# A hybrid decoder block: the mixer's projections in three products of high and low halves, and the recurrence's gate products inside the second branch

## The reference, cut to what matters

```python
h = rmsnorm(x, norm_mix_g)
q, k, v, xr, yr, ga, gl = split_cols(h @ w_in)      # 512, 128, 128, 512, 512, 1024, 1024
y_attn = sliding_window_attention(rope(q), rope(k), v, sinks) @ w_attn_o
xr = causal_depthwise_conv(xr, conv_w, conv_b)
r, i = sigmoid(xr @ w_rg + b_rg), sigmoid(xr @ w_ig + b_ig)   # 64-wide diagonal blocks
log_a = -8 * r * softplus(-lam)
h_t = exp(log_a) * h_{t-1} + sqrt(1 - exp(2 * log_a)) * (i * xr)
y_lru = (h_t * gelu(yr)) @ w_lru_o
x = x + (sigmoid(ga) * y_attn + sigmoid(gl) * y_lru) @ w_out
x = x + moe(rmsnorm(x, norm_ffn_g), ...)             # top 4 of 32 experts
return rmsnorm(x, norm_final_g)
```

## Time and profile before

| | before |
|---|---|
| median of three runs | 2228.98 us (2228.72 to 2231.96) |
| the profiled execution, its own time | 2230.49 us |
| its span in the trace | 2228.9 us |
| busy: PE / PEld / DVE / ACT / POOL | 94% / 67% / 70% / 56% / 13% |
| mean granted clock of TensorE | 0.97 |

### The profile page before, as it was taken

The page is one execution under the profiler, slowest core; times in us unless marked ns, Lnnn a source line. Parts: engine busy times, 40 slices in busy tenths (PEclk is TensorE's granted clock), DMA queues, the critical chain, the costliest instruction groups (busy, mean ns, idle before and its releaser), DMA issues.

```text
span 2228.9 us, 36027 instructions
## 1 busy us (share of the span) xinstructions
PE 2088.0 (94%) x11352; PEld 1494.9 (67%) x11353; DVE 1550.9 (70%) x1964; ACT 1244.1 (56%) x1655; POOL 291.4 (13%) x334
## 2 busy tenths in 40 slices
PE   7989988999989749999999999999999999999993
PEld 4445555767668637777777777777777777777772
DVE  4326654555443448878877778987877998977894
ACT  3152434334333336766766657766766776765674
POOL 3010000000002420211212200111210110220000
PEclk9998999999999869999999999999999999999997
DMA  7110020110143476988988779978979979977994
GB/s 225 38 38 0 22 76 1 38 39 1 38 151 133 142 196 224 371 284 287 377 282 282 256 260 380 373 270 291 370 259 325 372 276 368 356 258 246 378 342 159
DMA packets 247678, 489.51 MB, mean 220 GB/s; under 512 B 19915, under 2 KB 29991, under 8 KB 247536
## 3 DMA queue, kind: packets, MB, share of 16 engines
q1 hardware_dynamic: 218768, 439.37, 54.7%
q0 software_dynamic: 21088, 49.35, 8.4%
q10 hardware_dynamic: 7776, 0.19, 0.2%
HBM read 461.01 MB, written 32.05 MB: 221 GB/s over the span
## 4 chain that ended last, share of the span: by engine, by line
PE 84%; DVE 5%; issue 4%; ACT 2%; DMA 2%; SPq 1%; POOL 0%; ACTq 0%; DVEq 0%; POOLq 0%
PE psum L650 14%; PE psum L651 14%; PE psum L654 14%; PE psum L667 8%; PE psum L423 5%; PE psum L548 5%; PE psum L536 3%; PE psum L538 3%; PE psum L531 3%; PE psum L638 2%; PE psum L447 2%; PE psum L491 2%; PE psum L593 1%; PE psum L617 1%; PE psum L594 1%
## 5 line engine op out<-in xcount | busy, mean ns | idle before, releaser
L1451 DVE TENSOR_TENSOR w_lo<-ring,w_hi 128x1024 fp32r<-128x1024 f32 x768 | 915.0, 1221 | 144.2 <-ACT w_hi L890 132.7
L890 ACT ACTIVATE w_hi<-ring 128x1024 fp32r<-128x1024 f32 x768 | 803.7, 1059 | 277.7 <-PE psum L654 269.0
L650 PE MATMUL psum<-w_hi,rows_hi 128*128 128x512 f32 x1024 | 422.6, 413 | 4.3 <-DVE rows_lo L1455 2.5
L651 PE MATMUL psum<-w_hi,rows_lo 128*128 128x512 f32 x1024 | 400.4, 391 | 0.0
L654 PE MATMUL psum<-w_lo,rows_hi 128*128 128x512 f32 x1024 | 316.6, 390 | 0.0
L650 PEld LDWEIGHTS psum<-w_hi,rows_hi 128*128 128x128 f32 x1024 | 194.1, 190 | 47.0 <-issue 10.5
L654 PEld LDWEIGHTS psum<-w_lo,rows_hi 128*128 128x128 f32 x1024 | 192.7, 188 | 41.3
L650 PE MATMUL psum<-w_hi,act_hi 128*128 128x512 f32 x512 | 219.9, 429 | 0.0
L651 PEld LDWEIGHTS psum<-w_hi,rows_lo 128*128 128x128 f32 x1024 | 193.5, 189 | 37.7
L651 PE MATMUL psum<-w_hi,act_lo 128*128 128x512 f32 x512 | 202.7, 396 | 0.0
L667 PE MATMUL psum<-ring,region_m 128*32 128x256 f32 x3072 | 174.2, 380 | 0.0
(11 more groups left out here) (286 smaller groups left out, 2596.0 us busy)
## 6 DMA issues: line engine op xcount, KB each, us to landing
ring<-in_w_gate_up_dram SPq DMA_DIRECT2D x128, 2048.0 KB, 15.9
ring<-in_w_down_dram SPq DMA_DIRECT2D x64, 2048.0 KB, 12.0
ring<-in_w_in_dram SPq DMA_DIRECT2D x9, 1024.0 KB, 8.2
ring<-in_w_in_dram SPq DMA_DIRECT2D x3, 2048.0 KB, 22.6
region_m<-in_x_dram SPq DMA_DIRECT2D x8, 512.0 KB, 9.7
ring<-in_w_out_dram SPq DMA_DIRECT2D x2, 2048.0 KB, 7.7
region_a<-in_x_dram POOLq DMA_DIRECT2D x8, 512.0 KB, 4.8
acc_rows<-region_a POOLq DMA_DIRECT2D x8, 512.0 KB, 2.9
```

The costliest lines, as they stand in the source:

```text
L650: mm(bank(i), hi[:, ks], wh, start=(k0 + q == 0), stop=False)
L651: mm(bank(i), lo[:, ks], wh, start=False, stop=False)
L890: act.activation(w_hi[:, n % NBUF, :], place[i][:, k0 * HALF:(k0 + 2) * HALF], ACT.Copy).then_inc(hi_done, 1)
L1451: v.tensor_tensor(out=w_lo[:, n % NBUF, :], in0=place[i][:, k0 * HALF:(k0 + 2) * HALF], in1=w_hi[:, n % NBUF, :].bitcast(f32), op=ALU.subt ...
```

## The change

The input, turned, is kept as two fp32r tiles hT_hi and hT_lo for the whole mixer, without the gain; the gain goes into the weights when these are split (`in_high`, `in_low`, for w_in's columns of xr, yr, k/v, q and the merge gates). So the merge gates no longer split the input again for each piece. Branches, q, k, v and the two output projections now go through `three`. The weights of xr are loaded between tiles 3 and 4, the first four xr groups (tokens 0 to 511) stand between the turns of tiles 4 to 7, and the weights of q are loaded only when all 32 groups are done. The 16 recurrence gate products are now n = 12 to 27, inside yr (8 to 11, 28 to 31). The decay stands inside step s = 1 of the attention's loop, the recurrence in s = 1 and 2. The output projections are split on the fly, in pieces p (16 for each j) through a ring of OBUF = 3 tiles. Staging the experts' biases (`bias_part`) moves from the merge gates' stage to w_out's.

```diff
+OBUF = 3
+RG_AT = 12
...
+            def three(dst, w_hi_, w_lo_, m_hi_, m_lo_, first, final):
+                mm(dst, w_hi_, m_hi_, start=first, stop=False)
+                mm(dst, w_hi_, m_lo_, start=False, stop=False)
+                return mm(dst, w_lo_, m_hi_, start=False, stop=final)
...
             sp.dma_start(wxr_sb, w_in_v[:, :, OFF_XR:OFF_XR + LW]).then_inc(wxr_in, 16)
+            tiles(NT // 2, NT)
             sp.dma_start(wyr_sb, w_in_v[:, :, OFF_YR:OFF_YR + LW]).then_inc(wyr_in, 16)
+            sp.wait_ge(branch_mm, 8)
+            sp.dma_start(wkv_sb, w_in_v[:, :, OFF_KV:OFF_KV + 2 * KVW]).then_inc(wkv_in, 16)
+            sp.wait_ge(branch_mm, 32)
             sp.dma_start(wq_sb, w_in_v[:, :, OFF_Q:OFF_Q + QW]).then_inc(wq_in, 16)
...
+            def in_high(dst, src, arrived):
+                act.wait_ge(arrived, 16)
+                for k in range(KD):
+                    act.activation(dst[:, k, :], src[:, k, :], ACT.Copy, scale=gmix[:, k:k + 1]).then_inc(in_hi_done, 1)
...
+            def out_high(p_):
+                r, th = p_ // 2, p_ % 2
+                j, k, q = r // 8, r // 2 % 4, r % 2
+                if p_ >= OBUF:
+                    act.wait_ge(o_mm, p_ - OBUF + 1)
+                if th == 0:
...
+                    act.activation(ow_hi[r % 2], (wao_sb, wlo_sb)[q][:, k, j * P:(j + 1) * P], ACT.Copy)
+                act.activation(o_hi[p_ % OBUF], (oT, lruT)[q][:, k, th * HALF:(th + 1) * HALF], ACT.Copy).then_inc(o_hi_done, 1)
...
+                if s == 1:
+                    decay()
                 if s >= 2:
                     b = s - 2
+                    if b == 0:
+                        act.wait_ge(lru_done, LM)
...
-                if s < LM:
-                    recur(s)
+                if s == 1:
+                    decay()
+                    recur(0)
+                    recur(1)
+                if s == 2:
+                    recur(2)
+                    recur(3)
...
+            def out_low(p_):
+                r, th = p_ // 2, p_ % 2
+                j, k, q = r // 8, r // 2 % 4, r % 2
+                dve.wait_ge(o_hi_done, p_ + 1)
+                if th == 0:
+                    cols = slice(j * P, (j + 1) * P)
+                    v.tensor_tensor(out=(wao_lo, wlo_lo)[q][:, k, cols], in0=(wao_sb, wlo_sb)[q][:, k, cols],
+                                    in1=ow_hi[r % 2].bitcast(f32), op=ALU.subtract)
+                v.tensor_tensor(out=o_lo[p_ % OBUF], in0=(oT, lruT)[q][:, k, th * HALF:(th + 1) * HALF],
+                                in1=o_hi[p_ % OBUF].bitcast(f32), op=ALU.subtract).then_inc(o_lo_done, 1)
```

More of the change, by code:

```diff
@@ L414, in _ @@
[L414 to L426 removed]
+                last.then_inc(xT_done, 1)
@@ L428, in _ @@
+            for t in range(NT // 2):
+                turn_x(t)
+            for t in range(NT // 2, NT):
+                branch(t - NT // 2)
+                turn_x(t)
+            for n in range(4, RG_AT):
+                branch(n)
+            n = RG_AT
             pe.wait_ge(bd_in, 64)
@@ L436, in _ @@
                         n += 1
+            for n in range(RG_AT + 16, 32):
+                branch(n)
             def project(b):
@@ new lines, in _ @@
+            gate_high(0)
+            gate_high(1)
+            for j in range(KD):
+                for k in range(2, KD):
+                    gate_high(j * KD + k)
+                for p_ in range(16 * j, 16 * j + OBUF):
+                    out_high(p_)
+                act.wait_ge(gate_mm, KD * (j + 1))
+                if j >= 1:
+                    act.wait_ge(merged_done, 2 * j)
+                for th in range(2):
+                    for q in range(2):
+                        act.activation(sgate[th][q], bank(2 * th + q), ACT.Sigmoid).then_inc(sgate_done, 1)
+                for p_ in range(16 * j + OBUF, 16 * (j + 1)):
+                    if p_ == 16 * j + 14 and j + 1 < KD:
+                        gate_high((j + 1) * KD)
+                        gate_high((j + 1) * KD + 1)
+                    out_high(p_)
@@ new lines, in _, with conv @@
+            then(v.memset(xr[:, :, 0:3], 0.0))
+            def conv(m):
+                dve.wait_ge(branch_out, 5 + m)
+                then(v.tensor_scalar(xc[:, m, :], xr[:, m, 3:3 + SEQ], convw[:, 3, m:m + 1], convb[:, m:m + 1], ALU.mult, ALU.add))
+                for c in (2, 1, 0):
+                    ins = v.scalar_tensor_tensor(out=xc[:, m, :], in0=xr[:, m, c:c + SEQ], scalar=convw[:, c, m:m + 1],
+                                                 in1=xc[:, m, :], op0=ALU.mult, op1=ALU.add)
+                    if c:
+                        then(ins)
+                    else:
+                        ins.then_inc(conv_done, 1)
```

421 lines of the change are left out of this document (222 added, 199 removed).

## The result

| | before | after |
|---|---|---|
| median | 2228.85 us (2228.14 to 2231.96, 4 runs) | 2256.63 us (2254.52 to 2259.27, 4 runs) |
| ratio after / before | | 1.0122, 95% interval 1.0105 to 1.014 |
| the profiled execution: own time, span | 2230.49, 2228.9 us | 2259.27, 2257.7 us |
| mean granted clock of TensorE | 0.97 | 0.957 |

A forecast was written before the change was run, and what follows sets the result against it. PE, 84% of the chain, was taken to bound the kernel. Terms 13.2 - 7.4 - 1 + 13.4 + 1.5 = +19.7 us gave 2249 us, range 2226 to 2268.

The forecast's parts named there:

- The four waits: PE idle 10 us near 50 us, about 6 for q's weights, 30 around 180 to 217, 0.2 us gaps in projection stages.
- Front and branches: Input turns and branch groups: PE starts at 22.1, waits 10.6 us behind ACT's 13 loads, all groups end at 141.3.
- q's weights: Before the first projection: 2 MB asked for only after all groups land 7.7 us after issue; PE waits 6 us.
- The recurrence: Decay and recurrence on DVE in the attention's first steps delay step s = 4 to 245.1 from 231.96: 13.2 us more.
- Steps 4 to 7: Later attention steps: each saves 1.51 us on q and 0.35 on k and v, -7.4 us together.
- The projection stages: Output projections, eight j: three-tile ring makes a stage 15.4 us against 13.73 before, +13.4 us in all.
- The +1.5 for the last j: Before w_out: the last j's merge has no next gate products to cover it, about +1.5 us.
- Pieces at PE's pace: Rival, projection stages: three tiles suffice if the round is under 2.04 us; stage 12.5 us, total 2226; chance 0.13.
- Gains and waits cancel: Rival, whole kernel: shorter waits at several places, so the change does nothing; 2229 us, chance 0.07.
- The clock: Rival, projection stages: gaps at each piece drop PE to half clock; stage 21.8 us, +51 us, 2300; chance 0.06.
- Loads at their slow price: Rival, front: the 13 loads take 21.95 us instead of 8.8; +13 us, 2262; chance 0.08.
- k and v at 0.227: Rival, k and v projections: 0.227 us a product, +2.3 us a block, +19 us, 2268; chance 0.06.

The follow-up runs named there:

- with its operands in time: Changed kernel plus early decay and scans, later small loads, q's weights in quarters, four piece buffers, three weight pieces: 2201.5 us, ratio 0.9868 to the kernel before.

## Why the prediction was right, and where its sizes were off

**The question it asked.** "Does PE still get its operands as fast as it multiplies?" was the right one. The products became as cheap as forecast, the gates' apart: branch products 0.227 us apart, a step of the attention 2.0 us shorter (forecast 1.86; k and v products start 0.12 us apart, forecast 0.13). The Trainium skill ("TensorE: Matmul & The Clock Gate", section "LDWEIGHTS (loading the stationary operand)") gives a load of 128 columns as 128 over 1.2, an estimate of 107 ns. The trace comes close to it, just above. The four waits that the prediction named are the four in the view of waits.

**Front and branches.** Measured, with the forecast in brackets: start 22.76 (22.1), last turn done at 50.7 (49.6), 13 loads in 7.9 us (8.8), restart at 59.44 (60.2), end of all groups 141.3 (141.3). Of the two prices of a load, that for empty queues held: 0.61 us each, forecast 0.68.

**q's weights.** Landing 8.3 us after issue (7.7), first product 151.4 (150.6), a wait of 7.1 us (6).

**The recurrence: +16.5 us, forecast +13.2.** The order on VectorE is as written down, and each piece has its forecast length (decay 10.2, pair of recurrences 9.4, softmax 9.9). The undersized term is TensorE's clock. The sum counted a cold restart for q, but not the longer one (24 products in 8.6 us, forecast 7.4), nor another after TensorE had waited 3.0 us for the rotation of block 0; by 176.5 us the forecast was 2.9 us behind. Another 0.8 us is a third restart, after the wait of 8.8 us at 219.56. The profiled execution is also a late one: in the six variants with the same front and attention, step s = 4 starts at 244.6 to 247.0 us (forecast 245.1), and this one has 248.5.

**Steps 4 to 7: -7.8, forecast -7.4.** The handover to the gates gave nothing (forecast -1): the gates start 8.9 us later, and that is 16.5 - 7.8 + 0.2.

**The projection stages: +19.2 us, forecast +13.4.** This is the mis-sized term. The stage itself takes 15.6 us, forecast 15.4: with a round of three engines and the sigmoids ahead of piece 3, as the working has it. It was shown, not only timed: two buffers cost 61 us more, four buffers with three weight pieces 22 less. What the working missed is that the second weight tile closes the same round, and, for about 4 of the 5.8 missing us, the sentence "The gates' products are the same in number and stay PE's". They did stay the same in number, but 96 of them take 22.3 us, not 21.8, whatever their order and whether or not the projections are split. Why is open. The +1.5 for the last j measured 0.2.

**The sum.** 16.5 - 7.8 + 0.2 + 19.2 + 0.2 + 0.5 (behind w_out's start) = 28.8 us between the two traces, where the forecast had 19.7. The terms were off by +3.3, -0.4, +1.2, +5.8, -1.3 and +0.5, so little was cancelled by luck; the range held because it was wide enough for 9 us.

**The rivals.** "Pieces at PE's pace" fell: a stage takes 15.6 us, not under 12.9. It becomes true with more buffers, nearly: 13.3. That is VectorE's pace, not PE's. "Gains and waits cancel" fell, since the interval of the ratio starts at 1.0105. The clock did not fall in the stages; the granted clock is 1.00 in a stage of the changed kernel, and in one with two buffers:

```profile
425.84:441.46 15.62, 13.00 (x49) 8.31 (x48) 11.59 (x23) 11.71 (x25) 0.00 (x0) 1.00 0.25 68
...
428.05:450.33 22.28, 12.95 (x49) 8.45 (x49) 12.36 (x25) 12.18 (x27) 0.00 (x0) 1.00 0.18 47
```

The Trainium skill (the same page, "A second HAM failure mode: psum-queue depth-cycling") describes a bf16 kernel in which frequent small idles swing the clock. The trace here disagrees: 32 to 55 idles of 0.2 to 2.4 us left it at its upper level, while single ones of 8.8 and 19.6 us took it down. Loads at their slow price, and k and v at 0.227, fell too.

**Costed at nothing.** The biases' conversion under w_out showed nothing: the rest of the program is 0.5 us longer.

## What to carry to other kernels

When an engine's products get cheaper, list what the other engines must now deliver in the shorter time, and in which order their lists have it: here the block of VectorE work placed behind a rotation cost 30 us, as much as the whole loss, while VectorE had idled 37 us just before. A ring's speed is the round over its smallest count, so look for every tile that is reused in the round, weights too, and test with one buffer fewer as well as one more. Repair waits before judging an arithmetic change: this one is 1.2% slower as made, and with its operands in time 1.3% faster.

## What the runs showed of the hardware

- **A wait costs more than its idle time.** A product behind a wait has its successor 0.34 us later where others have 0.23. The view of waits does not count these 0.11 us; with the 55 waits of the kernel with two buffers they are 6 us.
- **Fetching a loop's instructions again.** The edit that puts 64 more waits ahead of the experts' loop brought 23 stalls of up to 6.8 us in it and 113 more packets of 16 KB on the queue that fetches instructions: 130 us, more than any edit here gained. The two kernels with the edit have it; the ten other experiments, the changed kernel and the kernel before do not, and they move no such packet at all from 1000 to 2200 us. The Trainium skill ("Runtime: NRT & Kernel Launch", section "Instruction fetch mechanics") says that instructions come in 16 KiB blocks and that a taken branch whose target is not in the current window makes the engine fetch it first. The trace agrees in the packet's size (2.34 MB / 143) and in the distance of the first long stalls, a pass of the loop. That the loop's position decides it is not shown: no run moves the loop without other edits.
- **GpSimd beside VectorE.** By the profile 128 x 128 subtractions on GpSimd took 0.46 to 0.91 us and made VectorE's 128 x 512 ones go from 0.68 to 0.77 us.
- **The clock and the length of a wait.** After waits of 2.4 us the granted clock stayed 1.00. After 7.1, 8.8 and 19.6 us the next products ran at the lower level (granted 0.50 from 59.44 to 65.00, and from 205.2 to 211.0). After 3.0 us, at 162.9, the first ones still ran at the upper level, and those from 164.1 to 167.3 at the lower one; TensorE had come back from that level only at 157.1.
